# Extra constant matmuls at the norms, three weight pieces prepared ahead for each feed-forward, and gated attention heads in another order

## What is computed

```python
def modulate_2(t, g, shift, scale):
    return rmsnorm(t, g) * (1.0 + scale[:, None, :]) + shift[:, None, :]

def swiglu_2(h, w_in, w_out):
    gate, up = jnp.split(h @ w_in, 2, axis=-1)
    return (jax.nn.silu(gate) * up) @ w_out

def step(state, inp):                                   # gated attention, one chunk of 64
    qi, ki, vi, gi = inp
    b = jnp.cumsum(gi, axis=-2)
    o_inter = jnp.einsum('bhck,bhkv->bhcv', qi * jnp.exp(b), state)
    diff = b[:, :, :, None, :] - b[:, :, None, :, :]
    decay = jnp.exp(jnp.where(causal, diff, -jnp.inf))
    attn = jnp.einsum('bhik,bhjk,bhijk->bhij', qi, ki, decay)
    o_intra = jnp.einsum('bhij,bhjv->bhiv', attn, vi)
    b_last = b[:, :, -1:, :]
    new_state = state * jnp.exp(b_last[:, :, 0, :])[..., None] + jnp.einsum(
        'bhck,bhcv->bhkv', ki * jnp.exp(b_last - b), vi)
    return new_state, o_inter + o_intra

x = x + g1[:, None, :] * y
h = modulate_2(x, norm_ffn[i], sh2, sc2)
x = x + g2[:, None, :] * swiglu_2(h, w_ffn_in, w_ffn_out)
```

## Time and profile before

| what | value |
|---|---|
| median of three runs | 1488.01 us (1482.47 to 1490.82) |
| profiled execution, its own time | 1484.64 us |
| its span (first to last instruction) | 1482.9 us |
| mean granted TensorE clock | 0.967 of full speed |
| TensorE matmuls (PE) | 9,993 records |
| VectorE (DVE) | 58% busy, 863.8 us |
| ScalarE (ACT) | 43% busy, 643.4 us |
| DMA | 270.00 MB, mean 182 GB/s |
| costliest line | L738, h by the high weights: 552.3 us in 1,824 matmuls |

### The profile page before, as it was taken

One profiled execution on the slowest core, in us unless ns is written; L12 is line 12 of the kernel. 1 busy time (PEld: TensorE's weight loads), 2 busy tenths in 40 slices (PEclk: granted clock), 3 DMA queues, 4 the chain that ended last, 5 costly groups with the idle time before them and its releaser, 6 DMA issues.

```text
span 1482.9 us, 26632 instructions
## 1 busy us (share of the span) xinstructions
PE 1389.9 (94%) x9993; PEld 1267.9 (86%) x9993; DVE 863.8 (58%) x1635; ACT 643.4 (43%) x1171; POOL 14.9 (1%) x81
## 2 busy tenths in 40 slices
PE   5999999999999899999799987999999999899997
PEld 2988889888888799999677776999997778899996
DVE  0576667666533377777555544777775432775553
ACT  3455545455322255444554422545532332545542
POOL 4000000000000000000000000000000000000000
PEclk9899999999999999999999999899999999899998
DMA  8655446454491178879676822688797264476562
GB/s 303 187 154 159 131 125 185 143 156 144 126 304 53 42 216 261 265 218 296 180 225 201 250 63 65 183 262 271 226 281 264 91 166 121 133 224 182 155 185 86
DMA packets 400019, 270.00 MB, mean 182 GB/s; under 512 B 9914, under 2 KB 357424, under 8 KB 399936
## 3 DMA queue, kind: packets, MB, share of 16 engines
q1 hardware_dynamic: 399936, 268.83, 61.1%
HBM read 267.75 MB, written 1.05 MB: 181 GB/s over the span
## 4 chain that ended last, share of the span: by engine, by line
PE 84%; DVE 8%; ACT 4%; issue 2%; DMA 2%; SPq 1%; DVEq 0%; ACTq 0%
PE bank L738 18%; PE bank L739 18%; PE bank L740 17%; PE bank L724 6%; PE bank L792 4%; PE bank L695 2%; PE bank L1117 1%; DMA big<-in_w_ada 1%; PE bank L710 1%; PE bank L917 1%; PE bank L918 1%; PE bank L910 1%; PE bank L689 1%; DVE w_low L1789 1%; DVE h_parts L1805 1%
## 5 line engine op out<-in xcount | busy, mean ns | idle before, releaser
L738 PE MATMUL bank<-h_parts,w_high 128*128 128x256 f32 x1824 | 552.3, 303 | 17.1 <-DVE h_parts L1805 15.2
L739 PE MATMUL bank<-h_parts,w_high 128*128 128x256 f32 x1824 | 525.0, 288 | 0.0
L740 PE MATMUL bank<-h_parts,w_low 128*128 128x256 f32 x1824 | 524.4, 287 | 0.0
L1789 DVE TENSOR_TENSOR w_low<-w_raw,w_high 128x1024 fp32r<-128x1024 f32 (+2 forms) x324 | 362.0, 1124 | 108.6 <-ACT w_high L1310 96.9
L738 PEld LDWEIGHTS bank<-h_parts,w_high 128*128 128x128 f32 x1824 | 358.0, 196 | 35.3 <-issue 25.2
L739 PEld LDWEIGHTS bank<-h_parts,w_high 128*128 128x128 f32 x1824 | 359.6, 197 | 3.8 <-issue 3.5
L740 PEld LDWEIGHTS bank<-h_parts,w_low 128*128 128x128 f32 x1824 | 358.7, 197 | 0.0
L1310 ACT ACTIVATE w_high<-w_raw 128x1024 fp32r<-128x1024 f32 (+2 forms) x324 | 312.9, 973 | 63.4 <-PE bank L740 18.0
L738 PE MATMUL bank<-act_parts,w_high 128*128 128x256 f32 x528 | 150.1, 284 | 0.0
L1302 ACT ACTIVATE evac<-bank 128x256 f32<-128x256 f32 x140 | 53.9, 385 | 219.9 <-PE bank L740 195.9
L740 PE MATMUL bank<-act_parts,w_low 128*128 128x256 f32 x528 | 148.6, 281 | 0.0
(11 more groups left out here) (345 smaller groups left out, 1577.8 us busy)
## 6 DMA issues: line engine op xcount, KB each, us to landing
ada_w<-in_ada_w SPq DMA_DIRECT2D x48, 1024.0 KB, 6.2
w_raw<-in_ffn_w_in SPq DMA_DIRECT2D x88, 512.0 KB, 3.9
w_raw<-in_w_in SPq DMA_DIRECT2D x72, 512.0 KB, 3.9
w_raw<-in_w_ffn_in SPq DMA_DIRECT2D x44, 512.0 KB, 4.0
ada_w<-in_w_ada SPq DMA_DIRECT2D x16, 1024.0 KB, 7.1
w_raw<-in_gla_w_in SPq DMA_DIRECT2D x24, 512.0 KB, 6.4
w_raw<-in_ffn_w_out SPq DMA_DIRECT2D x32, 384.0 KB, 4.1
w_raw<-in_ffn_w_out SPq DMA_DIRECT2D x32, 320.0 KB, 3.6
```

What stands on the lines that cost most here:

```text
L738: pe.matmul(acc[:, 0:T], hi[:, n, :], x_parts[:, k, 0, :], start=k == 0, stop=False)
L739: pe.matmul(acc[:, 0:T], hi[:, n, :], x_parts[:, k, 1, :], start=False, stop=False)
L740: mm = pe.matmul(acc[:, 0:T], lo[:, n, :], x_parts[:, k, 0, :], start=False, stop=k == kb - 1)
L1789: dve.tensor_tensor(w_low[:, s, 0:m], w_raw[:, s, 0:m], w_high[:, s, 0:m].bitcast(F32), ALU.subtract)\
```

## The change

It has three parts. **Constant products.** A function `fill(n)` on TensorE issues n matmuls of the matrix of ones with 512 columns of the constant `halves` into bank 5; nothing reads the result and they wait for nothing. One stands ahead of the last two sums of norms 1, 4 and 6 and of the norm that ends each feed-forward (2, 5 and 7); three stand behind norms 1, 4 and 6 ahead of the feed-forward, three ahead of and three behind norm 3; one more behind the second feed-forward, four behind the third.

```diff
+            def fill(n):
+
+                for _ in range(n):
+                    pe.matmul(bank[5][:, :], ones[:, :], halves.rearrange("p l c -> p (l c)")[:, 0:512], start=True, stop=True)
...
+            fill(1)
             norm_sum(1, range(KB - 2, KB))
+            fill(3)
```

```diff
-                for i in range(2):
-                    hidden(i)
+                pe.wait_ge(S("evacuated"), st_f.block0 + 3)
+                for k in range(KB):
+                    for j in range(3):
+                        split_product(st_f, 0, j, bank[j], h_parts, IN_PARTS[0], KB, ready=("h_low", parts_made) if j == 0 else None, part=[k])
+                split_product(st_f, 0, 3, bank[3], h_parts, IN_PARTS[0], KB)
+                hidden(1)
...
+                    if j % 2 and j < 6:
+                        high(st_f, 0, j // 2, IN_PARTS)
...
-                act.wait_ge(S("gemm_done"), st_f.block0)
-                high(st_f, 0, 0, IN_PARTS)
                 norm(n)
+                high(st_f, 0, 3, IN_PARTS)
...
-                    if f % 4 == 3:
-                        high(st_f, 0, f // 4 + 1, IN_PARTS)
```

```diff
-                pe.wait_ge(S("scaled2"), 15 * (n - 1) + 2)
+                pe.wait_ge(S("scaled2"), 15 * (n - 1) + 1)
...
-                pe.wait_ge(S("scaled2"), 15 * n)
                 pe.wait_ge(S("tok2"), 2 * n)
-                for t in range(NT):
-                    for l in range(LEVELS):
-                        pe.matmul(bank[3 + t][:, l * CHUNK:(l + 1) * CHUNK], kt[:, l, tok[t]], qt[:, l, t, :], start=True, stop=True)
-                    mm = pe.matmul(bank[3 + t][:, 2 * T - 1:2 * T], qk2[:, tok[t]], ones[:, 0:1], start=True, stop=True)
-                mm.then_inc(S("att_done"), 1)
-
                 for c in range(2):
                     r = slice(c * CHUNK, (c + 1) * CHUNK)
                     if c == 1:
                         pe.wait_ge(S("kv_done"), 3 * (n - 1) + 1)
                     pe.matmul(bank[6][:, c * T:(c + 1) * T], kd_tok[r, 0, :], v_tok[r, 0, :], start=True, stop=True).then_inc(S("kv_done"), 1)
-                products(G2)
+                pe.wait_ge(S("scaled2"), 15 * n)
+                for t in range(NT):
+                    for l in range(LEVELS):
+                        pe.matmul(bank[3 + t][:, l * CHUNK:(l + 1) * CHUNK], kt[:, l, tok[t]], qt[:, l, t, :], start=True, stop=True)
+                        if t * LEVELS + l < NT * LEVELS - 1:
+                            products(1 if (t * LEVELS + l) % 3 < 2 else 0)
+                    mm = pe.matmul(bank[3 + t][:, 2 * T - 1:2 * T], qk2[:, tok[t]], ones[:, 0:1], start=True, stop=True)
+                mm.then_inc(S("att_done"), 1)
                 rows2(3)
                 if not gemm:
...
+                if not gemm:
+                    for j in range(3):
+                        high(st_f2, 0, j, IN_PARTS)
...
+                if gemm:
+                    decays(n + 1)
...
+                    for j in range(3):
+                        low(st_f2, 0, j, IN_PARTS)
...
+                if gemm:
+                    dve.wait_ge(S("state2"), 3 * n)
+                    decays(i + 1)
```

More of the change, by code:

```diff
@@ L1593, in _, with decays @@
             act.activation(gl_a, gl_a, ACT.Ln, bias=1.0).then_inc(S("gate_act"), 1)
+            def decays(n):
+                act.wait_ge(S("expo"), 14 * n)
+                act.activation(expo, expo, ACT.Exp, scale=1.0 / TAU).then_inc(S("expo_done"), 1)
             def head2(i, gemm, chain, last=False):
@@ L2119, in ffn @@
                 h_low(n, KB - 1, h_parts)
-                for j in (1, 2):
-                    low(st_f, 0, j, IN_PARTS)
                 first = FFN_OF[n] * FB
@@ L2334, in _ @@
             softmax(st_h3.n - 1)
+            for j in range(3):
+                low(st_f3, 0, j, IN_PARTS)
             add_pairs(st_o3, 4 + 2 * KB)
```

68 lines of the change are left out of this document (45 added, 23 removed).

## The result

The changed kernel takes 1499.26 us (median of 6 runs, 1494.54 to 1501.17), the kernel before 1486.55 on the same chips (6 runs, 1482.47 to 1490.82): 1.0091 times as long, interval 1.0072 to 1.0110. It is 12.7 us slower where I forecast 0.8 more on the profiled execution and called it no change. The profiled execution took 1494.54 us with a span of 1492.8, 9.9 more than that of before.

What follows compares the result with a forecast made beforehand. TensorE, busy 94% of the span, was taken to bound the kernel. Terms -15.0 - 2.9 - 1.2 + 14.0 + 1.9 + 4.0 gave +0.8 us: 1485.4 profiled, 1488.8 as the median forecast, range 1475 to 1502.

Steps and rivals of the forecast that it cites:

- no change: Forecast case for the whole kernel: 1488.8 us, within 7.4 us (about 0.5%) of the kernel before; chance 0.50.
- heads cost more: Rival at each gated head's last key-value matmul: two low stretches per wait, dear type changes; sum +10.8, 1499; chance 0.15.
- A: Three feed-forward openings: TensorE no longer waits for h parts, constant products hold the clock; -15.0 us (-5.6 - 4.7 - 4.7).
- B: Between second feed-forward and latent projection: constant products in the norm's gaps remove the low clock; -2.9 us, bounds -2.9 and 0.
- C: End of the program: four constant products cover the chain to the last transposes; -1.2 us, bounds -1.9 and 0.
- E: Gated heads: early decays -6.7, exponential ahead of output norm +1.4, uncovered state waits +19.3; +14.0 us, bounds +9 and +16.
- F: Gated heads: changing operand types, 21 more returns at 0.08 us each; +1.9 us taken, bounds 0 and +5.9.
- G: Clock in the gated heads: five longer waits bring low stretches, 6.8 us paid becomes 10.8; +4.0, bounds -6.8 and +10.
- the signs that I had named for being wrong: Short waits at the heads' last key-value matmuls, low clock in an opening, or heads under 150 or over 172 us.
- If they don't hold the clock: Rival at the openings: constant products fail to hold the clock, three block-sets run at half speed; +17.9, 1506; chance 0.07.

Runs made afterwards that it cites:

- the version with all three edits: Changed kernel with the second halves' wait back, TensorE's gated-head order as before, VectorE's three fourth-head weight pieces behind the states: 1462.48 us, ratio 0.9841.

## Why the prediction was right or wrong

The number was too low by 10.5 us against the measured median, and "no change" was wrong; the time lies in the range, near the 1499 of the rival "heads cost more", but that is luck in the main. Of that rival, the longer low stretches came (6.8 or 10.2 us at each state wait), yet with TensorE idle in part of them; the dear change of type did not. And 10 of the missing us came from the feed-forwards, where it has nothing. By terms, on the profiled executions:

| term | forecast | measured | from |
|---|---|---|---|
| A openings | -15.0 | -4.8 | -2.53, -3.51, -3.17, the second halves' +0.05, +1.58, +2.20, and 0.2 ahead of each |
| B latent projection | -2.9 | -1.1 | 137.39 to 136.31 |
| C end | -1.2 | -1.3 | 24.97 to 23.69 |
| E waits in the heads | +14.0 | +14.7 | states +19.6, kd -6.2, output +1.3 |
| F changes of type | +1.9 | +0.2 | 0.59 us for a pair of both, 0.58 apart, 24 times |
| G clock in the heads | +4.0 | +4.8 | busy time at the low clock from 20.5 to 30.0 us, halved: +6.5 in the heads (13.6 to 26.6), -1.7 for one stretch less at the products ahead of them |
| untouched start | 0 | -2.9 | 504.58 to 501.71 |
| sum | +0.8 | +9.6 | of 9.9 |

**A is the step that failed**, in what it left out. It says "Behind the opening the pieces of the next four blocks come in time" and stops there, so that everything behind stands at nothing. What it says holds; the pieces that came late are those of the second half, 130 us on, held by a wait that the change itself puts into `high`. That took 6.4 us of waits and, with the low clock behind two of them, 10 of the 15 us. I had read the line for the streams it names and not for those that fall into its other branch. With that wait back the term is -15.3, against -15.0; from first product to fourth copy it is 11.85 us where I had 12.0. None of the signs that I had named for being wrong came (the openings at the high clock, the waits as long as forecast, the heads 162.0 us, between 150 and 172): they all looked where I had calculated.

**Inside A, a reason was wrong although the sum fits.** "If they don't hold the clock [...] A shrinks to some -2" is refuted: without the constant products the openings lost 5.4 us more, not 13, and with the constant products alone they gained 2.7. The gain comes from TensorE no longer waiting for parts and pieces. For the clock either one did most: of 28.3 busy us at the low clock in the openings the constant products alone left 2.9, the dense openings alone 12.3, both together none.

**B** was right where it looked. The latent projection's first 48 matmul records, before and after:

```profile
1136.66 17.72 PE L1117 MATMUL bank<-ring,hT 128*128 128x384 f32 x48 [2.25 <-ACT hT L1297]
...
1149.69 14.87 PE L1135 MATMUL bank<-ring,hT 128*128 128x384 f32 x48 [1.39 <-ACT hT L1318]
```

The next matmul began at 1154.22 before and at 1164.39 after, so they took 17.56 and 14.70 us, 2.86 less against the -2.9 forecast. (The wait ahead is shorter only because a constant product stands in it.) But 11 us on, TensorE waits for VectorE's sums for a modulation row, where it did not wait before:

```profile
1175.43 1.05 PE L690 MATMUL bank<-ones,scratch 128*128 128x1 f32 x8 [1.65 <-DVE scratch L1805]
...
1172.26 3.11 DVE L1805 SCALAR_TENSOR_TENSOR scratch<-ada_w,cact,scratch 128x512 f32<-128x512 f32 x4 [1.32 <-DMA ada_w<-in_ada_w]
```

VectorE, which waits there for the row's weights from memory, began these four sums 22.6 us after the projection's first matmul, and 22.0 us after it before (1158.64), so it had not become faster. Most of what the clock gave was waited away there; B stopped at the projection as A did at the openings.

**E was right in each number**: the states +19.6 where I had 19.3, kd -6.2 for -6.7. The state waits were each a chain of VectorE minus what stands behind attention on TensorE. Where I could not see the price, the exponential ahead of the Ln, the estimate of 1.4 measured 1.3.

**F** had the change of type right on one side (0.20 us) and missed the other: the matmul that is changed from gets shorter by as much. The Trainium skill's rule (TensorE: Matmul & The Clock Gate, section "Architectural detail: the array is 16× 32×32, not 1× 128×128") that weight loads are pulled ahead of running matmuls had given nothing for it, and the sum agrees with it.

**G** has nearly the right sum partly by luck. In the heads it is +6.5, not +4.0: the low stretches were longer than one or two (37.5 us in the five, where I had 25), though part of the waits lay inside them. One stretch less ahead of the heads, which the term did not cover, hides that.

## What to carry to other kernels

Work between attention and the product that needs its result is cover; before work is moved to a place where nothing is waited for, add up the other engine's chain behind the new last matmul, minus what is left there. When a change rewrites a wait in a helper, list every caller that falls into each branch, also the ones far down the program. When a stage gets shorter, look for the next thing that another engine or a transfer has to bring. And a stretch at the low clock costs half of its busy time only if TensorE sets its pace: an opening that goes at the pace of its parts has to be made dense first.

## What was not expected of the hardware

A float32 matmul of 64 columns takes 0.22 us in a run of its kind and 0.14 in front of a split product, whose first matmul then takes 0.20 instead of 0.12; alternating costs nothing. Waits of 4.72 us came with low stretches of 6.8, and such of 5.71 and 7.19 with 10.2, in the same stage of the changed kernel in which the wait of 2.65 had none. The length of a wait does not settle it, though: in the version with all three edits a stretch of 3.4 us began in one of the 2.65 us waits (898.09), and the same wait had none in others. And with the constant products alone the clock stayed high in two of three old openings, where three matmuls come every 0.79 us, and these stages were as long as before within 1.8 us. Which of the constant products does this was not tried one by one.
